# Strassen's seven products for eleven weight pieces of the two dense streams of an fp32 two-block network

## The reference, cut to what matters

```python
def trunk_layer(x, ctx, c, c_ctx, p, ang_r, ang_c, need_ctx):
    h  = x * (1.0 + scale[:, None, :]) + shift[:, None, :]
    hc = ctx * (1.0 + scale_c) + shift_c
    (a_q, a_k, a_v, a_g, g_q, g_k, g_v, g_af, g_ab, g_g,
     s_u, s_v, s_g, m_a, m_g, m_s) = jnp.split(h @ p['w_in'], pts, axis=-1)
    ...                                    # the same of hc
    y_attn = blocked_attention(ql, k_all, v_all) * jax.nn.silu(a_g)
    ...                                    # gated linear attention (GLA) scans, both directions
    y_gla = gla_finish(ol_f + flip(ol_b), p['gla_o_norm'], x.dtype) * jax.nn.silu(g_g)
    y_sgu = sgu(s_u, s_v, ...) * jax.nn.silu(s_g)
    m = (jax.nn.sigmoid(m_a) * (y_attn @ p['w_br_attn']) + jax.nn.sigmoid(m_g) * (y_gla @ p['w_br_gla'])
         + jax.nn.sigmoid(m_s) * (y_sgu @ p['w_br_sgu']))
    out = m @ p['w_out']
    ...
```

## Time and profile before

| what | value |
|---|---|
| median of three runs | 1561.46 us (1561.01 to 1563.44) |
| the profiled execution | 1564.0 us |
| its span, first to last instruction | 1562.2 us |
| TensorE busy | 1516.4 us, 97% |
| VectorE, ScalarE, GpSimd busy | 681.1, 415.0, 281.9 us |
| mean granted TensorE clock | 0.995 of full |
| weights and inputs read from HBM | 181.95 MB |

### The profile page before, as it was taken

How to read it: one execution, slowest core, us unless ns; L and a number is a source line. 1 busy time by engine, 2 the same in 40 slices (tenths; PEclk the granted TensorE clock), 3 DMA queues, 4 the chain that set the end, 5 groups by cost and what they waited for, 6 DMA issues and landing times.

```text
span 1562.2 us, 19171 instructions
## 1 busy us (share of the span) xinstructions
PE 1516.4 (97%) x7888; PEld 1077.2 (69%) x7888; DVE 681.1 (44%) x1460; ACT 415.0 (27%) x814; POOL 281.9 (18%) x314
## 2 busy tenths in 40 slices
PE   6999999999999999999999999999999999999997
PEld 2544544455688885555877888588888758888873
DVE  1233433464633343523344311365687216568721
ACT  1122325232312210121235320134233213423320
POOL 0322210131455441113002102110100011010010
PEclk9999999999999999999999999999999999999999
DMA  8642222300122231322322243423221323332231
GB/s 362 262 175 108 108 108 108 135 27 17 65 81 81 97 123 68 150 108 97 119 108 108 102 156 120 175 102 144 109 110 71 147 115 149 126 112 106 88 128 40
DMA packets 17370, 184.22 MB, mean 118 GB/s; under 512 B 2306, under 2 KB 2818, under 8 KB 4740
## 3 DMA queue, kind: packets, MB, share of 16 engines
q1 hardware_dynamic: 17284, 183.01, 30.7%
HBM read 181.95 MB, written 1.05 MB: 117 GB/s over the span
## 4 chain that ended last, share of the span: by engine, by line
PE 89%; ACT 3%; DVE 3%; issue 2%; DMA 1%; POOL 1%; SPq 0%; POOLq 0%; ACTq 0%; DVEq 0%
PE ps L756 86%; PE ps L811 3%; DVE arena L1749 1%; DVE arena L1755 1%; DMA arena<-in_wf 1%; POOL arena L2362 1%; ACT arena L1333 1%; ACT L1709 0%; ACT L1707 0%; DVE arena L1752 0%; ACT arena L1577 0%; ACT arena L1707 0%; ACT arena L1593 0%; ACT L1595 0%; ACT L1593 0%
## 5 line engine op out<-in xcount | busy, mean ns | idle before, releaser
L756 PE MATMUL ps<-arena 128*128 128x256 f32 (+7 forms) x7396 | 1467.1, 383 | 33.8 <-DMA arena<-in_wf 12.3
L756 PEld LDWEIGHTS ps<-arena 128*128 128x128 f32 (+5 forms) x7396 | 1023.6, 178 | 445.4 <-issue 311.9
L2362 POOL TENSOR_TENSOR arena<-arena 128x256 f32<-128x256 f32 (+6 forms) x254 | 247.3, 994 | 825.8 <-DVE arena L1755 409.3
L1755 DVE SCALAR_TENSOR_TENSOR arena<-arena 128x256 f32<-128x256 f32 (+4 forms) x470 | 231.0, 545 | 143.4 <-ACT arena L1475 38.8
L1333 ACT ACTIVATE arena<-ps 128x512 f32<-128x512 f32 (+2 forms) x280 | 134.9, 505 | 448.3 <-PE ps L756 370.5
L1749 DVE TENSOR_TENSOR arena<-arena 128x512 f32<-128x512 f32 (+14 forms) x190 | 140.4, 761 | 170.9 <-ACT arena L1333 95.8
L1755 DVE SCALAR_TENSOR_TENSOR arena<-arena,ps 128x256 f32<-128x256 f32 (+2 forms) x121 | 54.0, 456 | 207.2 <-PE ps L756 96.9
L1749 DVE TENSOR_TENSOR arena<-ps,arena 128x512 f32<-128x512 f32 (+16 forms) x120 | 48.8, 434 | 106.0 <-PE ps L756 97.3
L811 PEld LDWEIGHTS ps<-arena 128*128 128x128 f32 x488 | 55.7, 141 | 29.4 <-issue 19.5
L811 PE MATMUL ps<-arena 128*128 128x128 f32 x488 | 71.5, 278 | 3.1 <-ACT arena L1611 1.5
L1752 DVE TENSOR_SCALAR arena<-arena 128x256 f32<-128x256 f32 (+9 forms) x181 | 62.8, 382 | 15.7 <-POOL arena L2362 10.8
(11 more groups left out here) (96 smaller groups left out, 294.4 us busy)
## 6 DMA issues: line engine op xcount, KB each, us to landing
arena<-in_wf SPq DMA_DIRECT2D x69, 2048.0 KB, 8.3
arena<-in_wf SPq DMA_DIRECT2D x22, 1024.0 KB, 6.5
arena<-in_wf SPq DMA_DIRECT2D x2, 1152.0 KB, 7.7
arena<-in_xinT SPq DMA_DIRECT2D x2, 1024.0 KB, 15.9
arena<-in_xin SPq DMA_DIRECT2D x4, 512.0 KB, 3.9
arena<-in_rp SPq DMA_DIRECT2D x2, 1024.0 KB, 8.2
arena<-in_consts SPq DMA_DIRECT2D x1, 1410.0 KB, 21.6
arena<-in_pa SPq DMA_DIRECT2D x2, 532.0 KB, 9.4
```

The source lines that it names most:

```text
L756: return e.matmul(o, l, r, start=start, stop=stop, skip_group_check=True)
L1755: return e.scalar_tensor_tensor(out=o, in0=x, scalar=s, in1=y, op0=op0, op1=op1)
L2362: return e.tensor_tensor(o, x, y, op)
```

## The change

Eleven pieces of the streams go over to seven products: gqk, gv, ag, gg, su in layer A0, and ag, gg, su, mg0, ms0, ma1 in A1. The four chunk steps of such a piece become the products (1, 2), (6, 7), (5, 4), (3). GpSimd's four weight sums are spread over two new entries: "w1" (sums 3 and 2) in the step before the piece, "w2" (sums 1, in place of a quarter of the piece, and 4) in its first step. VectorE makes the four input sums once per layer, in the first step of the first such piece. The sums are kept in units 4 to 6 of the ring: while the loads from a0gqk to a0su and from a1ag to a1ma1 are placed, the ring has four units. Both order strings are new.

```diff
+SEVEN = [[("gqk", "A"), ("gv", "A"), ("ag", "T"), ("gg", "T"), ("su", "A")],
+         [("ag", "T"), ("gg", "T"), ("su", "A"), ("mg0", "G"), ("ms0", "G"), ("ma1", "G")]]
...
+    "daddddaadaddaddddaaadddaagaadggaddgdggdgadaggagaagadgdgggddagdagaagdddaggdggaadaggaaagdagagadgaagdgadaadaaa"
+    "gagagdaagdgdaggdgaadgaagadgaagagdadgaadgaadaadagdgadaadadadaaggagadgagaaggaadgagagaadadagggagggdg",
+    "dddaaaddddaddadgaaggdddadgddgdgdddadgdddadgdgagadaggdadadadagdggagagdgagdggagaadggdadggadadaddgaggdgdgagdadgad"
+    "daggddgdaggadadaagdggdgaggdagdggdaggdggagaaggdadaadaggdagdgaggdggdgddggd"]
...
+    for name, kind in SEVEN[l]:
+        i = [s[:1] for s in steps].index([(name, 0, "T" if kind == "T" else "A")])
+        for k in range(4):
+            steps[i + k] = [(name, x[0], "W" + kind) for x in WINOGRAD[2 * k:2 * k + 2]]
+        steps[i - 1] = steps[i - 1] + [("w1", name, "-")]
+        steps[i] = steps[i] + [("w2", name, "-")]
...
+        rest = Mem(arena, 4 * UNIT)
+        HW = [{n: rest.take(1024) for n in "1234"}]
+        WW = [{"2": r3(rest.take(1024), 4), "4": r3(rest.take(1024), 4), "3": r3(X[:, 1024:2048], 4)}]
...
+        short = [("a0gqk", "a0su"), ("a1ag", "a1ma1")]
...
+            for l in range(2):
+                if name == short[l][0]:
+                    rest_free[l] = [done_with[x] for x in tenant[4:] if x]
+                    tenant[4:], ends[l] = [f"rest{l}"] * 3, 4
+            units = max(ends) or NU
+            at = at if at + k <= units else 0
...
+            def one_of_seven(l, n, x):
+                w = use(f"a{l}{n}", 8)
+                _, s, t, _ = WINOGRAD[[y[0] for y in WINOGRAD].index(x)]
+                if x in (1, 2, 7):
+                    b = bank("dense", l, n, x)
+                else:
+                    b = psum("dense", l, n, 7 if x == 4 else 1)
+                    p.wait_ge(dense_act(l, n, {6: 1, 5: 6, 4: 7, 3: 5}[x]))
...
+                m = 128 if l else 256
+                for c in range(2):
+                    for k in range(4):
+                        w_c, h_c = (H[:, k, c], W[:, k]) if n == "gv" else (W[:, k, 128 * c:128 * c + 128], H[:, k])
+                        ins = mm(b[:, m * c:m * c + m], w_c, h_c, x in (1, 2, 7) and c == k == 0, k == 3)
...
+            def seven_sums(l, n, x, kind):
+                if x == 1 and n == SEVEN[l][0][0]:
...
+                    for i, (y, a1, a2) in enumerate(((o["1"], h12, h11), (o["2"], h22, o["1"]), (o["3"], h22, h12),
+                                                     (o["4"], h21, o["2"]))):
...
+            def seven_weights(l, n, first):
...
+                if first:
+                    g.wait_ge(pieces[name][2])
+                    make("3", w11, w21, ALU.subtract, 7)
+                    g.wait_ge(seven_sum(l, n, "3"))
+                    make("2", w22, WW[l]["3"], ALU.subtract, 6)
+                else:
+                    make("1", w21, w22, ALU.add, None)
+                    g.wait_ge(seven_sum(l, n, "2"))
+                    make("4", w12, WW[l]["2"], ALU.subtract, 3)
```

More of the change, by code:

```diff
@@ L292, in build_program @@
         BR = r3(X, 4)
+        rest = Mem(arena, 4 * UNIT)
+        HW = [{n: rest.take(1024) for n in "1234"}]
+        WW = [{"2": r3(rest.take(1024), 4), "4": r3(rest.take(1024), 4), "3": r3(X[:, 1024:2048], 4)}]
+        assert rest.at <= NU * UNIT
+        rest = Mem(arena, 4 * UNIT)
+        HW.append({n: rest.take(512) for n in "1234"})
+        WW.append({n: r3(rest.take(1024), 4) for n in "234"})
+        EW = [X[:, 0:512], rest.take(256)]
+        assert rest.at <= NU * UNIT
         SPARE = [[X[:, 512 * c:512 * c + 512] for c in range(4)],
@@ L375, in build_program @@
         DENSE = [dense_a(l) for l in range(2)]
-        FLAT = [[g for step in s for g in step if g[0] != "hx"] for s in DENSE]
+        FLAT = [[g for step in s for g in step if g[0] not in ("hx", "w1", "w2")] for s in DENSE]
         FIRST = [("pf", 0, "A"), ("pf", 1, "A"), ("ps", 0, "V"), ("ps", 1, "V"), ("pf", 2, "A"), ("pf", 3, "A"),
@@ L648, in build_program @@
         done_with = piece_done()
+        for l in range(2):
+            done_with[f"rest{l}"] = dense_act(l, SEVEN[l][-1][0], 3)
         pieces, at, off, tenant, count = {}, 0, 0, [None] * NU, [0] * NU
+        short = [("a0gqk", "a0su"), ("a1ag", "a1ma1")]
+        ends = [0, 0]
+        rest_free = [None, None]
         for name, w in PLAN:
             k = -(-w // UNIT)
-            at = at if at + k <= NU else 0
+            for l in range(2):
+                if name == short[l][0]:
[3 more added lines that the diff above has]
+            at = at if at + k <= units else 0
             count[at] += 16
@@ L656, in build_program @@
             tenant[at:at + k] = [name] * k
-            at, off = (at + k) % NU, off + 128 * w
+            at, off = (at + k) % units, off + 128 * w
+            for l in range(2):
+                if name == short[l][1]:
+                    ends[l] = 0
         def weights(name, k):
@@ new lines, in seven_copies, with event, tanh @@
+            def seven_copies(l, n, x, kind, last_th):
+                k = [y for y, _ in SEVEN[l]].index(n)
+                scale = 0.125 if n == "gqk" else 1.0
+                def event(y):
+                    return dn_act.hit(l, BY_ACT[l][(n, y)])
+                def tanh(f, t, src, last_th):
+                    q = f"{f}{t}"
+                    if kind == "WT":
+                        a.wait_ge(last_th)
+                    if q != "12":
+                        a.wait_ge(dense_dve(l, n, {"11": 2, "22": 5, "21": 4}[q]))
+                    o = two_chunks(l, TH) if kind == "WT" else seven_result(l, n, f, t)
+                    e.activation(o, src, ACT.Tanh, scale=0.5).then_inc(event("t" + q if q != "12" else 3), 1)
+                    return dense_dve(l, n, "g" + q) if kind == "WT" else None
+                if x in (2, 4):
+                    if x == 4 and kind != "WA":
+                        last_th = tanh(2, 2, seven_result(l, n, 2, 2), last_th)
+                    return last_th
+                a.wait_ge(dense_done(l, n, x))
+                b = two_chunks(l, psum("dense", l, n, 7 if x == 7 else 1), n)
+                if x == 1:
+                    copy(seven_result(l, n, 1, 1), b, scale=scale).then_inc(event(1), 1)
+                elif x == 6:
+                    copy(seven_result(l, n, 2, 1), b).then_inc(event(6), 1)
+                elif x == 7:
+                    if k:
+                        a.wait_ge(dense_dve(l, SEVEN[l][k - 1][0], 5))
+                    else:
+                        a.wait_ge(dense_dve(0, "ps", 3), *rest_free[l])
+                    copy(two_chunks(l, EW[l], n), b).then_inc(event(7), 1)
+                    if kind != "WA":
+                        last_th = tanh(1, 1, seven_result(l, n, 1, 1), last_th)
+                elif x == 5:
+                    copy(seven_result(l, n, 2, 2), b).then_inc(event(5), 1)
+                elif kind == "WA":
+                    copy(seven_result(l, n, 1, 2), b, scale=scale).then_inc(event(3), 1)
+                else:
+                    last_th = tanh(2, 1, seven_result(l, n, 2, 1), last_th)
+                    last_th = tanh(1, 2, b, last_th)
+                return last_th
```

143 lines of the change are left out of this document (123 added, 20 removed).

## The result

The changed kernel takes 1573.76 us (median of six runs, 1570.44 to 1580.38) against 1561.86 for the kernel before in the same comparison (1558.37 to 1563.44): ratio 1.0084, 95% interval 1.0058 to 1.0109. That is 12 us slower where I had forecast 14 us faster, and outside my range.

What follows compares the result with a forecast made beforehand. TensorE, busy 97% of the span, was taken as the bound. 24.4 us saved less 6.0 (loads), 1.5 and 1.3 (GpSimd's order) and 1.5 (hand-overs) gave 14.1: 1561.46 to 1547.4 us, 8-in-10 range 1538 to 1556.

Steps and rivals of the forecast that it cites:

- The work taken away: TensorE's matmul records in eleven pieces: 16.5 us saved in layer 0, 7.9 in layer 1, together 24.4 us.
- rival 4: Weight loads of 128-column records don't hide among other work; half of them bare costs 34 us more, 1581 us; chance 0.02.
- Loads: Ring cut to four units: five layer 0 pieces wait 8.7 us each, mostly covered by other steps; 6.0 us lost.
- rival 1: Attention and GLA steps cover the loads awaited in layer 0; 1539 us; chance 0.20.
- Rival 3: Attention and GLA steps don't run during layer 0's loads, TensorE stops there; slower, 1573 us; chance 0.08.
- GpSimd's order: Weight sums queued ahead of GLA levels delay L0 by 1.5 us; sums late at layer 1's start cost 1.3.
- Hand-overs: Copies, additions and input sums between products on ScalarE and VectorE are covered; 1.5 us for 77, ends 0 and 8.
- Rival 2: Hand-overs leak: in-order ScalarE and VectorE hold the next product, 10 us more lost; 1557 us; chance 0.17.
- The clock: TensorE's clock was taken as full throughout but for short dips, and given no term.
- The 160 us without a gap: Stretch of layer 0's later seven-product pieces, TensorE busy 160.00 of 160.00 us: taken to show such pieces run without gaps.

Runs made afterwards that it cites:

- e1: Changed kernel with GpSimd's 44 weight sums cut to 8 of 256 columns, products reading raw quarters, all waits kept: 1541.67 us, ratio 0.9876.
- e10: Changed kernel with VectorE making weight sums; A0's scan step behind gv's first step, A1's sums 3 and 2 one step earlier: 1546.55 us, ratio 0.9909.
- e7: Kernel before the change with only the new order strings of both streams: 1564.72 us, ratio 1.0028.
- e6: Changed kernel with VectorE instead of GpSimd making the 44 weight sums, in the piece's first step and behind product 2's addition: 1559.96 us, ratio 0.9996.

## Why the prediction was wrong, step by step

- **The work taken away: right.** 24.4 us forecast; with the sums small (e1), TensorE's busy time is 26.6 us below, for the same records as in the changed kernel. Part of that is clock (0.999 in that execution, 0.995 before): 14.6 us lie in the first window, where 16.5 were forecast, 9.1 in the second, where 7.9 were (6.7 by e10's window, which has a slow stretch behind A0's merge as the kernel before has and e1 has not), and 2.9 where nothing was changed. So it is 21 to 24 us. Records of 128 columns cost 0.112 us among other work too (16 of them 1.787 us), as in the earlier trace rows, so rival 4 didn't happen.
- **Loads: 6.0 us forecast, 1.4 waited for in A0's stream, 0.4 once VectorE keeps up.** They landed in 8.4 us as the earlier trace rows say. At the first four boundaries TensorE has 8.4, 9.1, 9.0 and 10.2 us from the last record of a piece to the first of the next, of which 7.1, 8.3, 8.0 and 9.8 are work, where I had summed 6.2, 7.7, 7.4 and 9.7: the steps cost more than their records by their mean, and hide the landing; and the pause of 0.8 us among them, before the query's transposes, comes with the new order in the dense kernel too (e7). On this step rival 1 was right. Rival 3 gave 1573 us, the number measured, by a mechanism that isn't there: no wait for a load in the streams is over 0.8 us. The agreement is luck.
- **GpSimd's order: 2.8 us forecast (1.5 at L0, 1.3 at A1's start).** L0 waited for VectorE by 0.5 us. As a direct wait it is nothing: not waiting for the sums changed nothing.
- **Hand-overs: the step that failed.** I wrote "Covered, unless ScalarE or VectorE stands in an attention or GLA step in order before it" and took 1.5 us for all 77. I had read from the earlier trace rows that VectorE and GpSimd slow one another, 3.3 us for 2.35 and 2.6 for 1.24, and charged that to the sums alone: GpSimd's four per piece and VectorE's four in layer 0. The price lies in everything that VectorE does between SBUF tensors while GpSimd is at work for 115 us more: key norms, the modulation's small sums, scans, gates, and in A1 the input sums, which I had not priced there (10.0 us for the four, against products of 1.8). Measured against e1: 22.4 us of idle time and 15.2 us more busy time, mostly at the slower clock behind the pauses; 20.8 and 11.9 of these in the two windows. Even the sums were priced too low: the 2.6 us in the earlier trace rows are the mean of one operation that was not kept out (1.2 us) and two that were (3.3), so "up to 2.6 us each" is wrong, and the four of that stretch took 11.1 us, not 10.4. The two ends that I gave the term, 0 and 8 us, didn't hold it, since both came from products counted evenly and none from VectorE's operations beside a sum. Rival 2 had the place (VectorE's and ScalarE's order) and not the cause or the size.
- **The clock: "I leave it alone".** It was full in the earlier trace rows, where TensorE hardly paused. I priced each pause at its length only. An estimate from the windows behind the changed kernel's four long pauses (busy time times what the granted clock lacks to 1) gives 9 us of lost speed for 15.9 us of pauses, more than half as much again.
- **The evidence I leaned on.** The 160 us without a gap in the earlier trace rows hold GpSimd's sums beside VectorE, and nothing late. It is the merge: no scans, no softmax, no norms in VectorE's order. It showed that seven products can run clean, not that they do among attention steps. And it held the price that I missed. By form, VectorE from 430 to 590 in the kernel before:

```profile
L1749 DVE TENSOR_TENSOR arena<-arena 128x512 f32<-128x512 f32 x25 | 30.0, 1224 | 50.4 <-ACT arena L1333 50.3
```

  One such operation takes 0.69 us alone; here TensorE had other work meanwhile.
- **The sum.** 24.4 - 10.3 = 14.1 forecast. In spans: -23.0 without contention (TensorE's busy time 26.6 less, 3.6 more idle), +37.6 by it, so +14.6. By medians, which the profiled executions of these kernels miss by up to 5 us: -19.6, +32.1, and +11.9 in the direct comparison. With VectorE making the sums in the right places the gain is 13.9 us (1560.45 to 1546.55; in spans 12.9, TensorE's busy time 19.1 less, 6.2 more idle): my 14.1 in number, from another kernel.

What stays open: how the loss divides between operations directly kept out and those late behind them; and why the order alone costs the dense kernel 4 us. In the profiled executions it is 1.8 us only, and no single pause shows it: A0's stream has five pauses of 0.6 to 0.8 us before transposes, where it had three of 0.6 to 0.7 before products and transposes.

## What to carry over

Work given to an engine that is 18% busy is not free if that engine shares a path with one that others wait for: list what the second engine runs in the same stretch, and price those operations too, not the added ones. A stretch that shows a scheme running clean is evidence only for stretches with the same neighbours on every engine. When TensorE is the bound and full, cost a pause of 4 us at its length and about half of that again for the slow clock behind it.

## What the runs showed of the hardware

- **Who is kept out.** In the changed kernel VectorE's tensor_tensor, scalar_tensor_tensor, tensor_scalar and scan operations with every tensor in SBUF stretch beside GpSimd's sums, whatever their size: scalar_tensor_tensor of 256 elements from 0.42 to 2.03 us, tensor_scalar of 256 elements from 0.35 to 2.5, a scan of 512 from 1.2 to 3.3. Those with an operand in PSUM, reduces and reciprocals don't. By form in A0's stream (75 to 400), first the changed kernel, then with small weight sums:

```profile
L1929 DVE TENSOR_SCALAR arena<-arena 128x256 f32<-128x256 f32 x16 | 8.8, 594 | 0.3
L2109 DVE TENSOR_TENSOR_SCAN arena<-arena 128x512 f32<-128x512 f32 x4 | 8.4, 2092 | 0.1
L1926 DVE TENSOR_TENSOR arena<-ps,arena 128x512 f32<-128x512 f32 x9 | 6.2, 689 | 11.1 <-PE ps L849 11.0
```
```profile
L1929 DVE TENSOR_SCALAR arena<-arena 128x256 f32<-128x256 f32 x16 | 5.0, 354 | 0.3
L2109 DVE TENSOR_TENSOR_SCAN arena<-arena 128x512 f32<-128x512 f32 x4 | 6.3, 1584 | 0.1
L1926 DVE TENSOR_TENSOR arena<-ps,arena 128x512 f32<-128x512 f32 x9 | 6.2, 689 | 18.5 <-PE ps L849 18.4
```

  The Trainium skill (SBUF — State Buffer, "SBUF: two separate sides") has the rule: the port pair of VectorE and GpSimd is an exclusive lock, held for a whole instruction, and a VectorE operation with two SBUF inputs or in a two-port mode is shut out by a GpSimd operation that reads SBUF and started first. These rows agree, and so do single operations: the scan of 3.26 us began 0.62 us after a sum of GpSimd and ended 1.1 us after that sum, about its own 1.23. The 4.58 us beside short GpSimd instructions go beyond "the whole instruction": there VectorE was passed over for five that began while it waited. The rule would have spoken against this change, and I did not weigh it.
- **The clock.** In the changed kernel granted clocks of 0.55 to 0.67 follow pauses of 3.7 to 4.5 us of a TensorE that had been busy throughout; behind its pauses of up to 1.5 us in the two streams the next product ran at full speed. Length alone doesn't decide: with the sums on VectorE (e6, e10) the granted clock is 0.6 in the 4 us behind the one pause of 1.5 us before the query's transposes, which followed work at full speed but for 0.3 us; and a pause of 2.5 us behind A0's merge, which every kernel here has, is followed by a slow stretch in the traces of both kernels and by none in e1's. Without the long pauses e1 runs at a mean of 0.997 to 0.999, the changed kernel at 0.986 to 0.992.
- **GpSimd's instruction size.** A sum of 1024 elements takes 2.35 us in one instruction and 4 x 0.72 in four; beside VectorE's input sums 3.3 and 4 x 1.7.
